# First transfers in finer pieces and another order, constants and pooling bands made by GpSimd

## The reference, cut to what matters

```
layer 0: proj = rms_norm(h) @ w_in_even          # 1024 x 2048: q | k | v | p
         ya = chunk_band_attention(q, k, v)      # 8 heads of 64, q and k normed per head, bias by distance
         yb = multiscale_pool(p) @ pool_w        # per 128-channel group: mean of the last 2, 4, 8 or 16 positions, minus itself
         h  = h + [ya, yb] @ w_out_even
layer 1: proj = rms_norm(h) @ w_in_odd           # 1024 x 2560: u | vv | q | k | v
         yc = gelu(u) * (tril(sgu_w) @ rms_norm(gelu(vv)) + b);  yd = stick_breaking_attention(q, k, v)
         h  = h + [yc, yd] @ w_out_odd
both:    h  = h + moe(rms_norm(h))               # 4 groups x 8 experts, SwiGLU, ff 256: top group, top 2 in it
```

## Time and profile before

| what | value |
|---|---|
| median of 3 runs | 587.52 us (586.75 to 589.58) |
| the profiled execution | 586.97 us, of which the span is 585.2 us |
| PE busy | 535.8 us (92% of the span), 3978 matmuls |
| PEld, DVE, ACT busy | 337.4, 182.3, 180.2 us |
| POOL busy | 6.5 us, 16 instructions |
| DMA | 236.20 MB, mean 404 GB/s |
| granted TensorE clock, mean | 0.974 |

### The profile page before, as it was taken

One profiled execution on the slowest core, in us unless ns is written; L12 is line 12 of the kernel. 1 busy time (PEld: TensorE's weight loads), 2 busy tenths in 40 slices (PEclk: granted clock), 3 DMA queues, 4 the chain that ended last, 5 costly groups with the idle time before them and its releaser, 6 DMA issues.

```text
span 585.2 us, 9373 instructions
## 1 busy us (share of the span) xinstructions
PE 535.8 (92%) x3978; PEld 337.4 (58%) x3978; DVE 182.3 (31%) x311; ACT 180.2 (31%) x341; POOL 6.5 (1%) x16
## 2 busy tenths in 40 slices
PE   6999999999999998687799999999999999987686
PEld 4888787465455545242478878874655455452423
DVE  3686954411011101010275466543111011010102
ACT  5844845021111111010394696551211110110101
POOL 0000000000000000000000000000000000000000
PEclk7999999999999999897999999999999999998989
DMA  8999999999999999999999995698999999999996
GB/s 309 433 426 417 423 418 422 394 427 429 427 426 427 423 427 428 428 426 417 425 422 429 421 392 181 260 422 347 429 426 424 428 429 424 427 427 428 426 417 236
DMA packets 23730, 236.20 MB, mean 404 GB/s; under 512 B 2624, under 2 KB 3648, under 8 KB 4864
## 3 DMA queue, kind: packets, MB, share of 16 engines
q1 hardware_dynamic: 22960, 232.06, 94.9%
q0 software_dynamic: 720, 3.45, 1.4%
HBM read 234.45 MB, written 1.05 MB: 402 GB/s over the span
## 4 chain that ended last, share of the span: by engine, by line
PE 62%; DMA 31%; ACT 4%; DVE 2%; issue 1%; SPq 0%; ACTq 0%
DMA raw<-stream 30%; PE psum L1357 13%; PE psum L305 8%; PE psum L306 8%; PE psum L307 8%; PE psum L1336 7%; PE psum L1413 6%; PE psum L1385 6%; DMA xT<-x_turned 1%; PE psum L1428 1%; PE psum L563 1%; ACT pb L602 1%; PE psum L1177 1%; PE psum L1394 1%; ACT whi L290 1%
## 5 line engine op out<-in xcount | busy, mean ns | idle before, releaser
L1357 PE MATMUL psum<-raw,x 128*32 128x512 f32 x688 | 91.1, 636 | 21.0 <-issue 12.0
L297 DVE TENSOR_TENSOR raw_lo<-raw,whi 128x1024 fp32r<-128x1024 f32 x52 | 62.4, 1222 | 40.0 <-ACT whi L290 39.9
L1413 PE MATMUL psum<-y,pickT 128*128 128x256 f32 x256 | 68.2, 398 | 0.0
L1336 PEld LDWEIGHTS psum<-pick,h 128*128 128x128 f32 x512 | 58.7, 192 | 16.4 <-issue 14.1
L305 PE MATMUL psum<-whi,hnT_hi 128*128 128x512 f32 x144 | 58.2, 404 | 6.6 <-DVE hnT_lo L409 4.7
L290 ACT CAST whi<-raw 128x1024 fp32r<-128x1024 f32 x52 | 53.1, 1047 | 33.5 <-PE psum L307 29.2
L1336 PE MATMUL psum<-pick,h 128*128 128x128 f32 x512 | 62.5, 279 | 1.0 <-DVE pick L1300 1.0
L1308 DVE TENSOR_TENSOR pick<-pick,lists 128x256 f32<-128x256 f32 x16 | 6.8, 424 | 179.6 <-PE psum L1428 179.6
L1413 PEld LDWEIGHTS psum<-y,pickT 128*128 128x128 f32 x256 | 44.7, 189 | 31.0 <-issue 27.0
L306 PE MATMUL psum<-whi,hnT_lo 128*128 128x512 f32 x144 | 57.9, 402 | 0.0
L307 PE MATMUL psum<-raw_lo,hnT_hi 128*128 128x512 f32 x144 | 57.4, 399 | 0.0
(11 more groups left out here) (215 smaller groups left out, 502.2 us busy)
## 6 DMA issues: line engine op xcount, KB each, us to landing
raw<-stream SPq DMA_DIRECT2D x55, 2048.0 KB, 36.0
raw<-stream SPq DMA_DIRECT2D x49, 1024.0 KB, 12.4
late<-stream SPq DMA_DIRECT2D x17, 2048.0 KB, 31.0
late<-stream SPq DMA_DIRECT2D x22, 1024.0 KB, 12.9
late_alone<-stream SPq DMA_DIRECT2D x2, 1024.0 KB, 9.8
raw<-stream SPq DMA_DIRECT2D x2, 512.0 KB, 5.7
xT<-x_turned SPq DMA_DIRECT2D x2, 512.0 KB, 7.7
h<-x SPq DMA_DIRECT2D x1, 1024.0 KB, 12.7
```

What stands on the lines that cost most here:

```text
L297: nc.vector.tensor_tensor(raw_lo[PLACE[c].place][:, cols], chunk(c)[:, cols], whi[:, n % SPLIT, cols].bitcast(F32), ALU.subtract).then_inc ...
L1336: mm = nc.tensor.matmul(psum[:, b, (k - ks[0]) * P:(k - ks[0] + 1) * P], h[:, t, k * P:(k + 1) * P], pick[:, t, :], start=(t == 0), stop=( ...
L1357: nc.tensor.matmul(psum[rows, b, :], lhs[:, rows], chunk(c)[:, e * W4:(e + 1) * W4], start=start, stop=stop).then_inc(moe_used, 1)
L1413: nc.tensor.matmul(psum[:, 4 + i, t * QUARTER:(t + 1) * QUARTER], pickT[:, t * P:(t + 1) * P], y[:, i % 2, :], start=(q == 0 and t == 0), ...
```

## The change

- **Start.** The constants given from HBM shrink from 618 to 170 columns. `xT` comes in four transfers of 256 KB, chunk 0 in four pieces of 512 columns (256 KB), chunk 1 in two halves, in the order in which they are used: `xT` part 0, pieces 0 and 1 of chunk 0, `xT` part 1, pieces 2 and 3, `xT` part 2, half 0 of chunk 1, `xT` part 3, half 1. x in rows comes behind chunk 2. `split_hi`, `split_lo` and TensorE's waits go by these pieces; ScalarE and VectorE take turned x before each part. TensorE does 14 matmuls on zeros and no longer waits for `cst`.
- **Squares.** ScalarE squares tile 0 of x (two instructions), VectorE tile 1 (a product and a reduction over 1024 columns) and the sum; the splits of chunks 2 and 3 stand around them.
- **Constants.** Identity, negative triangle and negative ones are made by GpSimd at the start (three memsets, two `affine_select`).
- **Biases.** The second query tile's bias loads only its left half (0.5 MB); the right half is copied by GpSimd from the first tile's. `pb1` is laid out by key tile first.
- **Bands.** GpSimd makes them behind its issue of the pool's weights (now 256 KB): four memsets, a copy, and for each of two parts one `affine_select` over all windows, four over one window each, and a subtraction. SyncE's wait for `pool_c` goes.
- **Second mixer.** Chunk `PROJ1` comes in two halves, and `split_hi` of its first half stands right behind `turned_hi` of block 0, ahead of the copy of the fourth `y`. `sgu` and `vgain` are issued when ScalarE has split the first half of chunk `PROJ1 + 3`.

The diff, cut to its core:

```diff
+PIECES = {0: ((0, 1), (1, 2), (2, 3), (3, 4)), 1: ((0, 2), (2, 4))}
+
+APART = tuple((c, first) for c in PIECES for first, _ in PIECES[c][:-1]) + ((PROJ1, 0),)
+
+
+def pieces_of(c):
+    return PIECES.get(c, ((0, 2), (2, 4)))
+
+
+def pieces_done(c, quarters):
+
+    n = 2 * mixer_no(c) + sum(len(PIECES[b]) - 2 for b in PIECES if b < c)
+    return n + 1 + sum(last < quarters for _, last in pieces_of(c))
...
+        def load_piece(sp, c, first, last):
+            cols = slice(first * W4, last * W4)
+            arrival = piece_landed[c, first] if (c, first) in APART else landed[PLACE[c].told_by]
+            sp.dma_start(chunk(c)[:, cols], from_stream(c)[:, cols]).then_inc(arrival, 16)
+
         def load_chunks(sp, chunks):
 
             for c in chunks:
                 place_free(sp, c)
             c = chunks[0]
-            if len(chunks) == 1:
+            if c == PROJ1:
+                for first, last in pieces_of(c):
+                    load_piece(sp, c, first, last)
...
+        def make_constants(pool):
+
+            nc.gpsimd.memset(ident, 0.0).then_inc(filled, 1)
+            nc.gpsimd.memset(negtri, -1.0).then_inc(filled, 1)
+            nc.gpsimd.memset(negones, -1.0).then_inc(made, 1)
+            pool.wait_ge(filled, 2)
+            nc.gpsimd.affine_select(out=ident, in_=ident, pattern=[[-1, P]], compare_op=ALU.not_equal, fill=1.0,
+                                    base=0, channel_multiplier=1).then_inc(made, 1)
+            nc.gpsimd.affine_select(out=negtri, in_=negtri, pattern=[[-1, P]], compare_op=ALU.is_ge, fill=0.0,
+                                    base=0, channel_multiplier=1).then_inc(made, 1)
+
         def keep_warm_pe(n):
...
-            pool.dma_start(pb[0][:], even_bias[:, 0:HEADS * P].rearrange("p (j k) -> p j k", j=HEADS)
-                           ).then_inc(ev.bias_landed, 16)
-            pool.dma_start(pb[1][:], even_bias[:, HEADS * P:].rearrange("p (j k) -> p j k", j=HEADS)
-                           ).then_inc(ev.bias_landed, 16)
+            for t, part in ((0, even_bias[:, 0:HEADS * P]), (1, even_bias[:, HEADS * P:])):
+                pool.dma_start(pb[t][:, 0], part.rearrange("p (j k) -> p j k", j=HEADS)).then_inc(ev.bias_landed, 16)
             pool.wait_ge(ev.bias_landed, 32)
 
-            nc.gpsimd.memset(pb[0][0:64, :, 64:128], NEG).then_inc(ev.bias_masked, 1)
-            nc.gpsimd.memset(pb[1][0:64, :, 192:256], NEG).then_inc(ev.bias_masked, 1)
+            nc.gpsimd.memset(pb[0][0:64, 0, :, 64:128], NEG).then_inc(ev.bias_masked, 1)
+            pool.wait_ge(ev.bias_masked, 1)
+            nc.gpsimd.tensor_copy(pb[1][:, 1], pb[0][:, 0]).then_inc(ev.bias_masked, 1)
             pool.wait_ge(ev.qk_turned, 4)
-            pool.dma_start(pool_c[:], even_pool).then_inc(ev.pool_c_landed, 16)
+            pool.dma_start(pool_w[:], even_pool).then_inc(ev.pool_w_landed, 16)
+            make_band(pool)
+
...
+            for n, cols in enumerate((slice(0, S), slice(S, S + P))):
+                width = cols.stop - cols.start
+                nc.gpsimd.affine_select(out=band[:, :, cols], in_=band[:, :, cols], pattern=[[0, 4], [1, width]],
+                                        compare_op=ALU.is_ge, fill=0.0, base=0, channel_multiplier=-1
+                                        ).then_inc(ev.band_cut, 1)
+                pool.wait_ge(ev.band_cut, 5 * n + 1)
+                for g, w in enumerate(WINDOWS):
+                    nc.gpsimd.affine_select(out=band[:, g, cols], in_=band[:, g, cols], pattern=[[-1, width]],
+                                            compare_op=ALU.is_ge, fill=0.0, base=w - 1, channel_multiplier=1
+                                            ).then_inc(ev.band_cut, 1)
+                pool.wait_ge(ev.band_cut, 5 * n + 5)
+                own = band[:, :, cols.start:cols.start + P]
+                nc.gpsimd.tensor_tensor(own, own, ident.unsqueeze(1).to_broadcast([P, 4, P]), ALU.subtract
+                                        ).then_inc(ev.band_ready, 1)
...
-            pe.wait_ge(ev.pool_c_landed, 16)
+            pe.wait_ge(ev.band_ready, 2)
...
-            keep_warm_pe(12)
-            pe.wait_ge(cst_landed, 16)
+            keep_warm_pe(14)
...
-            split_hi(act, 0, (0,))
-            turned_hi(act, 0, hnT_hi0, (0, 1))
-            split_hi(act, 0, (1,))
-            turned_hi(act, 0, hnT_hi0, (2, 3))
-            split_hi(act, 1)
-            square_act(act, 0, 0, x_landed, 0)
-            square_act(act, 0, 1, x_landed, 0)
+            for b, (c, part) in enumerate(((0, 0), (0, 1), (1, 0), (1, 1))):
+                turned_hi(act, 0, hnT_hi0, (b,))
+                split_hi(act, c, (part,))
+            split_hi(act, 2)
+            square_act(act, 0, 0, x_landed, 0, (0,))
+            square_act(act, 0, 1, x_landed, 0, (0,))
+            split_hi(act, 3, (0,))
             rms_act(act, 0)
-            split_hi(act, 2)
-            split_hi(act, 3)
+            split_hi(act, 3, (1,))
             block_out(act, 0, PROJ0, 0, q_in)
             split_hi(act, 4, (0,))
...
-            split_lo(dve, 0, (0,))
-            turned_lo(dve, 0, hnT_hi0, hnT_lo0, (0, 1))
-            split_lo(dve, 0, (1,))
-            turned_lo(dve, 0, hnT_hi0, hnT_lo0, (2, 3))
-            split_lo(dve, 1)
+            for b, (c, part) in enumerate(((0, 0), (0, 1), (1, 0), (1, 1))):
+                turned_lo(dve, 0, hnT_hi0, hnT_lo0, (b,))
+                split_lo(dve, c, (part,))
+            split_lo(dve, 2)
+            dve.wait_ge(x_landed, 16)
+            link(nc.vector.tensor_tensor(x_squared[:], h[:, 1, :], h[:, 1, :], ALU.mult))
+            link(nc.vector.tensor_reduce(ssq[:, 1:4:2], x_squared[:].rearrange("p (n d) -> p n d", n=2), AX.X, ALU.add))
+            ss_dve(dve, 0)
+            split_lo(dve, 3, (0,))
             rstd_dve(dve, 0)
-            split_lo(dve, 2)
-            split_lo(dve, 3)
+            split_lo(dve, 3, (1,))
             head_squares(dve, q_in, 0, 2)
             split_lo(dve, 4, (0,))
...
-            pool.wait_ge(moe_used, EACH * (PER_QUAD * SPILL_AT + 1))
+
+            pool.wait_ge(hi_done, pieces_done(PROJ1 + 3, 2))
             pool.dma_start(sgu[:], odd_sgu).then_inc(od.sgu_landed, 16)
-            pool.wait_ge(norm.lo_ready, 5)
             pool.dma_start(vgain[:], odd_vgain.partition_broadcast(P)).then_inc(od.vgain_landed, 16)
...
-            split_hi(act, PROJ1, (0,))
...
+                        split_hi(act, PROJ1, (0,))
...
-            sp.dma_start(cst[:], consts).then_inc(cst_landed, 16)
-            sp.dma_start(chunk(0)[:, 0:HALF_CH], from_stream(0)[:, 0:HALF_CH]).then_inc(first_landed, 16)
-            sp.dma_start(xT[:, 0:4, :], x_turned[:, 0:4, :]).then_inc(xT_landed[0], 16)
-            sp.dma_start(chunk(0)[:, HALF_CH:CH], from_stream(0)[:, HALF_CH:CH]).then_inc(landed[0], 16)
-            sp.dma_start(xT[:, 4:8, :], x_turned[:, 4:8, :]).then_inc(xT_landed[1], 16)
-            load_chunks(sp, (1,))
+            sp.dma_start(cst[:, C_GIVEN:], consts).then_inc(cst_landed, 16)
+            for b, pieces in enumerate((((0, 0, 1), (0, 1, 2)), ((0, 2, 3), (0, 3, 4)), ((1, 0, 2),), ((1, 2, 4),))):
+                sp.dma_start(xT[:, XT_PARTS[b], :], x_turned[:, XT_PARTS[b], :]).then_inc(xT_landed[b], 16)
+                for piece in pieces:
+                    load_piece(sp, *piece)
+            load_chunks(sp, (2,))
             sp.dma_start(h[:], x_in.rearrange("a (t p) d -> p (a t) d", p=P)).then_inc(x_landed, 16)
-            for chunks in TRANSFERS[2:]:
-                if chunks[0] == RAW + 3:
-                    sp.wait_ge(ev.pool_c_landed, 16)
+            for chunks in TRANSFERS[3:]:
                 if chunks[0] == BEHIND:
```

121 lines of the change are left out of this document (68 added, 53 removed).

## The result

The changed kernel takes 584.2 us (median of 11 runs, 581.55 to 586.07) against 587.47 (11 runs) of the kernel before on the same chip: ratio 0.9933, 95% interval 0.9918 to 0.9948. In a later set the same kernel gave 583.2 against 587.87, ratio 0.9925 (0.9908 to 0.9943). By these ratios, which lie near those of the means, it is 3.9 to 4.4 us less, with about 0.9 us of uncertainty either way; the medians differ by 3.3 and 4.7 us. Forecast was 4.65 us less and 582.9. Its profiled execution took 584.33 us with a span of 582.6 (before 585.2).

The account below looks back on a forecast made before the run. Bytes bound the kernel until 290.6 us, TensorE in the second mixer, bytes again from about 400 us. 4.25 - 0.6 + 1.0 = 4.65 us off the profiled 586.97 gives 582.3, as median 582.9; range 580.6 to 585.8.

Parts of the forecast that it names:

- TensorE's start: Kernel's beginning: first real matmul at 6.7 us instead of 10.58, clock staying up; net 4.4 us earlier (3 to 5.5).
- Bands: GpSimd makes the bands from 43.9 us in 9 us (7 to 14), before TensorE needs them at 57.5.
- Cost nothing: Claim that GpSimd's making of the bands is hidden by the last projection block and adds no time.
- The doubled 9 us: Case of GpSimd's band work doubled by contention with VectorE: reaches 62 us, 4.4 late, some 3.4 us over forecast.
- The dry stream: SyncE's lack of places before 106.93 us: whether transfers run out of issued work; claimed no pause, no recovery counted.
- cover: Transfer work still left when SyncE issues again after its lack of places near 105 us; forecast 3.95 us.
- releases earlier by 4.4 us: At SyncE's lack of places near 105 us, TensorE was to free places 4.4 us sooner, as at its start.
- rival "dry stream": TensorE gains 2 us instead of 4.4, so 2 us of stream are lost near 105 us: 584.9; chance 0.12.
- Bytes and small pieces: Transfers before `PROJ1`: 1.804 MB fewer save 4.25 us; smaller pieces at the start cost 0.6 us.
- this rival: First 256 KB transfers run at the slow rate of 4 to 8 us, costing 3.2 us, not 0.6: 585.5; chance 0.12.
- Entry of the second mixer: `PROJ1` in halves, split earlier: TensorE starts the second mixer at 292.1 instead of 293.07, 1.0 us gained (0 to 1.2).
- signs of being wrong: TensorE idle before band matmuls, DMA share under 0.9 (15 to 340 us), under 300 GB/s (4 to 12 us), longer second mixer.

Follow-up runs that it names:

- the runs with either part alone: Two runs: the changed kernel with its start put back as before, ratio 0.9956; the kernel before with only the new start put in, ratio 1.0004.
- two queues: Changed kernel with the four quarters of chunk 0 issued by ScalarE's queue beside SyncE's, same sizes and bytes: 584.56 us, ratio 0.9937.
- the bands loaded: Changed kernel with the bands loaded from memory again (1 MB with pool weights) and SyncE's wait for them put back: 584.74 us, ratio 0.995.

## Why the prediction was nearly right, step by step

**TensorE's start: right in kind, 1 us short.** First real matmul at 7.69 us (6.7 forecast; 6 to 7.5 was to show it right), clock 1.00 as forecast. Constants and the first part of `xT` were to be there at 3.8 us. The constants were (at 2.8 us, 1.9 from issue); `xT` was first used at 5.12 us, 3.9 us after its issue, where the 2.8 us of the earlier trace rows had been assumed. The wait for chunk 1 was 1.0 us in this profile and 1.6 in the next, for 1.4. Lead at q's turn 3.29, not 4.4. (The prediction's steps to the first low part add up to 5.8, not 5.9; it had no effect, as the warm matmuls were to end later.)

**Bands: right, but not free.** 45.56 to 56.3 us is 10.7 us, inside 7 to 14, and TensorE had no wait for them. "Cost nothing" failed: they and VectorE hold each other up, which took 0.5 us of TensorE's lead. The Trainium skill, GPSIMD Engine Reference, Specifications, says that the two share their interfaces to the on-chip memory and contend when VectorE has two inputs there. The trace agrees: 1.86 instead of 1.23 us. The doubled 9 us that the prediction drew from it did not come, since VectorE's splits leave GpSimd alone most of the time.

**The dry stream: the step that failed.** It is the cover's term "releases earlier by 4.4 us" that was mis-sized, and with it the "no pause". The prediction had the lead of 4.4 us against 3.65 us of saved stream, so cover 3.95 us and no loss. The lead at B was 2.76 and 2.28 us in the two profiles. With that its own formula gives 3.2 - 3.65 + 2.76 = 2.3 us, less than the 3.2 at which the kernel before lost 0.5 already. The stream did dip (382 GB/s), and D then follows the lead: 2.76 + 0.6 for `sgu` = 3.4, measured 3.3 and 2.9 (288.3 to 285.0 and 285.4), where 3.65 was forecast. (The 0.6 is an estimate from bytes, as said above.) So the rival "dry stream" was partly there, in a mild form: 2.5 us of lead instead of its 2, and 0.35 to 0.75 us of the stream's 3.65 gone instead of 2. That the start is what makes the saved bytes count was right, and is shown by the runs with either part alone.

**Bytes and small pieces.** Saved bytes as counted: the page shows 234.66 MB against 236.20. The pieces cost 0.38 MB by 14 us, 0.9 us at 424 GB/s, for 0.6; in the eight other such profiles 0.46 to 0.57 MB, 1.1 to 1.3 us. Put into the sum by themselves (4.25 less 0.9 to 1.3) they would give 2.95 to 3.35 us, and 3.3 and 2.9 were measured, so this rival explains the number as well as the lead does. Other runs speak against it as the whole cause: without the new start 4.24 MB had been moved by 14 us, with two queues 4.00, more than in the changed kernel, and both landed later at D, by 1.5 and 1.9 us. How the shortfall of the changed kernel itself divides between the two is not shown.

The Trainium skill, DMA: Bandwidth & Descriptors, Bandwidth, wants at least 1 MiB in a transfer for 75% of peak. The trace agrees for the first microseconds, 151 and 308 GB/s in the two windows up to 8 us, and not for 8 to 15 us, where pieces still went and 396 GB/s were moved. The 341 GB/s for 1 MB in the same section of the Trainium skill is below what this stream of 1 and 2 MB transfers moves when many are queued (425 GB/s from 200 to 290 us).

**Entry of the second mixer: right in size, not wholly kept.** 1.0 us was forecast. From the last down matmuls to the entry it is 1.1 us less with halves than with the whole chunk. Of this E - D shows 0.9 us in the second profile of the changed kernel, but 0.2 in the first. How it came is a little different: TensorE stood behind its own down matmuls, not behind the split. ScalarE split at 286.71 and TensorE began at 289.60 (286.68 and 289.29 in the second profile), both just outside the 285 to 286.5 and 288 to 289 named.

**The rest.** That `sgu` and `vgain` behind `PROJ1` cost nothing was right: from the entry to the router's last product it is 102.33 us, before 102.31. Of the signs of being wrong none came in the windows read: TensorE had no wait ahead of the band matmuls, 340 GB/s were moved from 4 to 12 us, and the DMA share was never under 0.9 there. The share of 1.0 between 95 and 120 us, which was to show it right, came too (1.00), and shows little: the rate within it dips to 382 GB/s, and before it was 1.00 as well.

**Sum.** TensorE enters the second mixer 3.5 and 3.8 us earlier in the two profiles: the stream's term is 3.3 and 2.9 of it, the entry's 0.2 and 0.9. The ratios give 3.9 and 4.4, each with 0.9 us of uncertainty, so they agree with both and with 4.65. By the traces the forecast was about 1 us too high: 0.35 to 0.75 us in the stream's term, the rest in the entry's. That the median of 584.2 lies so near 582.9 is in part luck, since behind the entry executions differ by up to 1.8 us.

## What to carry to other kernels

Where a stream of weights goes through a fixed number of places, ask at its tightest point which is late, the bytes or the releases: a saving moves the end only as far as the later of the two moves, so fewer bytes and an earlier engine must be made together, and their sum cannot be read from either alone. A lead won at the start is not kept: follow it through each later chain (here 3.29, 3.25, 2.76 us) before it is used in a sum. And work that is "hidden" on GpSimd can still lengthen VectorE's instructions with two inputs in on-chip memory; look for who waits behind the one that it meets.

## What the hardware showed that was not expected

- Where VectorE's instruction has two inputs in on-chip memory and GpSimd's reads there, the two take turns by whole instructions: the one that starts first runs at its own speed, and the other ends about when both would have ended one after the other (to some 0.15 us in the pairs shown). Memsets of GpSimd (split 1.22 us beside them) and VectorE's additions from the matmul banks (0.68 us beside selects and alone) were not stretched. GpSimd's copy of 1024 columns took 2.09 us when it began 0.03 us behind VectorE's `k_in` (1.23 us), and with the bands loaded it began 0.16 us ahead of it: then the copy took 1.04 us and `k_in` 1.96. These are the two orders, the changed kernel first:

```profile
40.01 1.23 DVE L631 TENSOR_TENSOR k_in<-k_in,stat 128x1024 f32<-128x1024 f32 x1
40.04 2.09 POOL L555 COPY pb<-pb 128x1024 f32<-128x1024 f32 x1
```

```profile
39.97 1.04 POOL L556 COPY pb<-pb 128x1024 f32<-128x1024 f32 x1
40.13 1.96 DVE L607 TENSOR_TENSOR k_in<-k_in,stat 128x1024 f32<-128x1024 f32 x1
```

- The branch to the overflow path, whose body these inputs never run, has TensorE stand 5.9 to 6.5 us in layer 0 in twelve profiles and 7.6 in one. The same call in layer 1 has 5.7 to 6.3 us in thirteen profiles and 8.0 in one. Taking it out in layer 0 took the stand away; what in it takes the time is open.
- Small first transfers: 151 to 203 GB/s from 2 to 4 us when SyncE alone issues them, 257 with two queues, and yet a first matmul 2.3 us later. The order in which the first bytes land counted for more than how many were moved.
